# Expert matmuls in plain fp32 on column tiles in place of a three-product split

## What is computed

```
hidden = silu(rows @ w_e_gate[l, e]) * (rows @ w_e_up[l, e])      # 1024 -> 1024
x[picked] += affinity * gate2 * (hidden @ w_e_down[l, e])          # 1024 -> 1024, scatter-add
```

## Time and profile before

| | us |
|---|---|
| median of 3 runs | 2853.08 (2852.55 to 2854.35) |
| profiled execution, its own time | 2853.54 |
| its span in the trace | 2851.5 |
| TensorE busy | 2629.6, 92% of the span |
| mean granted TensorE clock | 0.972 of 2.4 GHz |

### The profile page before, as it was taken

One profiled execution on the slowest core, in us unless ns is written; L12 is line 12 of the kernel. 1 busy time (PEld: TensorE's weight loads), 2 busy tenths in 40 slices (PEclk: granted clock), 3 DMA queues, 4 the chain that ended last, 5 costly groups with the idle time before them and its releaser, 6 DMA issues.

```text
span 2851.5 us, 40451 instructions
## 1 busy us (share of the span) xinstructions
PE 2629.6 (92%) x13576; PEld 1829.0 (64%) x13576; DVE 1933.7 (68%) x2986; ACT 1628.2 (57%) x2399; POOL 477.1 (17%) x359
## 2 busy tenths in 40 slices
PE   7899999999997999999979989999999599999995
PEld 1487676766773666666648767776677366666663
DVE  7743566444357999999955356644535799999995
ACT  6635544454324777777743554544422477777774
POOL 1030002112301211212013000211231112122121
PEclk9899999999998999999989999999999899999997
DMA  9630112121447999999972111211134599999995
GB/s 362 250 93 31 34 44 72 41 67 45 168 162 281 383 379 380 381 376 377 385 243 80 43 34 38 73 47 49 63 130 173 208 375 378 377 384 380 378 383 184
DMA packets 191183, 593.74 MB, mean 208 GB/s; under 512 B 23628, under 2 KB 33674, under 8 KB 191054
## 3 DMA queue, kind: packets, MB, share of 16 engines
q1 hardware_dynamic: 171646, 527.68, 49.9%
q0 software_dynamic: 19408, 64.37, 7.6%
HBM read 566.73 MB, written 25.23 MB: 208 GB/s over the span
## 4 chain that ended last, share of the span: by engine, by line
PE 76%; DVE 9%; ACT 6%; issue 6%; DMA 3%; POOL 0%; ACTq 0%; SPq 0%; DVEq 0%; POOLq 0%
PE bank L530 22%; PE bank L532 20%; PE bank L531 20%; PE bank L941 4%; PE bank L969 3%; DVE low L1554 2%; ACT high L1179 2%; PE bank L956 2%; DMA ring<-in_w_mod 1%; DVE st L1858 1%; PE bank L725 1%; DMA U<-x_normed,idx_g 1%; DVE sigr L1781 1%; PE bank L1090 1%; PE bank L1128 1%
## 5 line engine op out<-in xcount | busy, mean ns | idle before, releaser
L1179 ACT ACTIVATE high<-ring 128x1024 fp32r<-128x1024 f32 (+1 forms) x976 | 1023.8, 1052 | 393.4 <-PE bank L532 359.9
L1994 DVE TENSOR_TENSOR low<-ring,high 128x1024 fp32r<-128x1024 f32 x736 | 880.6, 1220 | 72.6 <-ACT high L1179 69.8
L530 PE MATMUL bank<-high,hT_high 128*128 128x512 f32 (+2 forms) x1280 | 516.5, 404 | 25.4 <-DVE low L1554 9.7
L531 PE MATMUL bank<-low,hT_high 128*128 128x512 f32 (+2 forms) x1280 | 484.3, 378 | 0.0
L532 PE MATMUL bank<-high,hT_low 128*128 128x512 f32 (+2 forms) x1280 | 483.4, 378 | 0.0
L530 PE MATMUL bank<-high,xeT_high 128*80 128x512 f32 x1056 | 419.0, 397 | 5.6 <-issue 3.5
L531 PE MATMUL bank<-low,xeT_high 128*80 128x512 f32 x1056 | 416.6, 394 | 0.0
L532 PE MATMUL bank<-high,xeT_low 128*80 128x512 f32 x1056 | 416.5, 394 | 0.0
L1554 DVE TENSOR_TENSOR low<-ring,high 128x1024 fp32r<-128x1024 f32 (+2 forms) x240 | 285.9, 1212 | 114.0 <-ACT high L1179 112.7
L530 PEld LDWEIGHTS bank<-high,hT_high 128*128 128x128 f32 x1280 | 242.3, 189 | 92.2 <-issue 17.2
L1400 ACT ACTIVATE att<-bank,st 128x640 f32<-128x640 f32 (+3 forms) x200 | 136.4, 682 | 278.9 <-DVE st L1863 220.9
(11 more groups left out here) (261 smaller groups left out, 3164.4 us busy)
## 6 DMA issues: line engine op xcount, KB each, us to landing
ring<-in_w_e_gate SPq DMA_DIRECT2D x256, 512.0 KB, 6.3
ring<-in_w_e_up SPq DMA_DIRECT2D x256, 512.0 KB, 7.0
ring<-in_w_e_down SPq DMA_DIRECT2D x256, 512.0 KB, 6.3
ring<-in_w_mod SPq DMA_DIRECT2D x64, 512.0 KB, 6.5
ring<-in_w_gate SPq DMA_DIRECT2D x64, 512.0 KB, 4.1
ring<-in_w_in SPq DMA_DIRECT2D x24, 512.0 KB, 4.6
U<-in_w_mod SPq DMA_DIRECT2D x20, 512.0 KB, 5.4
ring<-in_w_branch SPq DMA_DIRECT2D x16, 512.0 KB, 4.4
```

What stands on the lines that cost most here:

```text
L530: nc.tensor.matmul(out, lhs[0], rhs_high, start=start, stop=False)
L531: nc.tensor.matmul(out, lhs[0], rhs_low, start=False, stop=False)
L1179: A(high[:, HSLOT[g], :, 0:w], ring[:, SLOT[g], :, 0:w], ACT.Copy).then_inc(high_done, 1)
L1994: V.tensor_tensor(low[:, SLOT[ahead], :, :], ring[:, SLOT[ahead], :, :], high[:, HSLOT[ahead], :, :].bitcast(F32), ALU.subtract).then_inc( ...
```

## The change

Experts no longer split their weights. TensorE multiplies the raw fp32 chunk in plain fp32, and the picked tokens are laid out in two ways over the array's columns: the 64 sample tokens stand in two halves of 64 columns, which take the two halves of a chunk, and the 16 prompt tokens, padded to 32, stand in four strips of 32 columns, which take the four quarters of 256 columns. A chunk is 2 + 4 matmuls in place of 6. Sample results lie in one PSUM bank (partitions 0 to 63 hold the first 512 output columns, 64 to 127 the rest), prompt results in 256 columns of another.

What follows from it: silu, the product and the hidden rows are on 128 partitions with 512 + 256 columns instead of 80 with 2 x 512; the hidden turn is six full transposes instead of eight; the turned rows are copied once by ScalarE, with no low part; the gate values are spread over 128 partitions by small VectorE operations and two more transposes before the stage; GpSimd zeroes the pad; the gate2 row is loaded in six pieces instead of two; the result of an expert is evacuated in two operations on 64 partitions by 512 and four on 16 by 256. The dense part keeps its splits, with four high slots.

```diff
@@ matrix (TensorE)
-                        split_done(g + k, i)
+                        pe.wait_ge(ring_full[SLOT[g + k]], i * (16 * LOOP_FILLS) + 16 * FILLS[g + k])
+                        w = ring[:, SLOT[g + k], :, :]
                         for half in range(2):
-                            ins = three(bank(first + half)[0:CAP, :], stat(k), high[:, HSLOT[g + k], half, :],
-                                        low[:, SLOT[g + k], half, :], k == 0, k == KD - 1)
+                            mm(bank(first)[CAP_S * half:CAP_S * (half + 1), :], stat(k)[0], w[:, half, :], start=(k == 0), stop=(k == KD - 1))
+                        for q in range(4):
+                            ins = mm(bank(first + 1, 0, QW)[STRIP * q:STRIP * (q + 1), :], stat(k)[1],
+                                     w[:, q // 2, QW * (q % 2):QW * (q % 2 + 1)], start=(k == 0), stop=(k == KD - 1))
                         ins.then_inc(ring_used, 1)
@@ hid_turn (TensorE)
-                            for k in range(4):
-                                kk = 4 * half + k
-                                ins = tr(bank(6 + half, k * CAP, (k + 1) * CAP), hid[0:CAP, kk * P:(kk + 1) * P], ident[0:CAP, 0:CAP])
+                            for k in range(4 if half == 0 else 2):
+                                ins = tr(bank(6 + half, k * P, (k + 1) * P), hid[:, half * NW + k * P:half * NW + (k + 1) * P], ident[:, :])
@@ before the first gather (TensorE)
                 pe.wait_ge(topT_ready, l + 1)
+                pe.wait_ge(spread_set, l + 1)
+                for a in range(2):
+                    ins = tr(bank(1, (2 + a) * NE, (3 + a) * NE), spread[:, a, :], ident[0:NE, 0:NE])
+                ins.then_inc(spread_tr, 1)
                 rows_turn(0, 16 * (NE // 2 * l + 1))
@@ experts (ScalarE)
-                    for j in range(6 * NQ):
...
-                        split_high(g + HIGH_E, i)
+                    g = g0 + CH_GATE0 + e * CH_EXP
+                    rows_copy(1 - e, n_exp * 2 + 2)
+                    hid_copy(0, n_exp)
+                    for half in range(2):
+                        silu(half, n_exp + 1, i * (2 * CH_EXP) + (g + 4 * NQ))
@@ before the stage (VectorE)
+                then(V.memset(spread[:, 1, :], 0.0))
+                for half in range(2):
+                    at = slice(CAP_S * half, CAP_S * (half + 1))
+                    V.tensor_copy(spread[:, 0, at], top_v[:, 0:CAP_S])
+                for q in range(4):
+                    at = slice(STRIP * q, STRIP * q + CAP_P)
+                    ins = V.tensor_copy(spread[:, 1, at], top_v[:, CAP_S:CAP])
+                ins.then_inc(spread_set, 1)
+                dve.wait_ge(spread_tr, l + 1)
+                V.tensor_copy(gate_T[:, :, :], bank(1, 2 * NE, 4 * NE).rearrange("p (a n) -> p a n", a=2)).then_inc(spread_done, 1)
@@ experts (VectorE)
-                        chunk_low(g + HIGH_E, i)
...
-                    y_half(0, e, i * (2 * CH_EXP) + (g + 1))
-                    y_half(1, e, i * (2 * CH_EXP) + (g + 1)).then_inc(y_ready, 1)
+                    for half in range(2):
+                        at = slice(CAP_S * half, CAP_S * (half + 1))
+                        V.scalar_tensor_tensor(out=ybuf[0:CAP_S, e, half * NW:(half + 1) * NW], in0=bank(first)[at, :],
+                                               scalar=gate_c[at, e, 0:1], in1=gate2_b[at, 0:NW], op0=ALU.mult, op1=ALU.mult)
+                    for q in range(4):
+                        at = slice(STRIP * q, STRIP * q + CAP_P)
+                        ins = V.scalar_tensor_tensor(out=ybuf[CAP_S:CAP, e, QW * q:QW * (q + 1)], in0=bank(first + 1, 0, QW)[at, :],
+                                                     scalar=gate_c[at, e, 1:2], in1=gate2_b[at, NW:NW + QW], op0=ALU.mult, op1=ALU.mult)
+                    ins.then_inc(y_ready, 1)
@@ before the first gather, and behind both gathers (GpSimd's queue)
+                G.memset(xeT[:, :, :, CAP:WIDE], 0.0).then_inc(pad_zero, 1)
...
-                pool.dma_start(gate2_b[0:CAP_S, :], mod_dram[l, 1:2, 5 * D:6 * D].broadcast_to([CAP_S, D])).then_inc(gate2_in, 16)
-                pool.dma_start(gate2_b[CAP_S:CAP, :], mod_dram[l, 0:1, 5 * D:6 * D].broadcast_to([CAP_P, D])).then_inc(gate2_in, 16)
+                for half in range(2):
+                    pool.dma_start(gate2_b[CAP_S * half:CAP_S * (half + 1), 0:NW],
+                                   mod_dram[l, 1:2, 5 * D + NW * half:5 * D + NW * (half + 1)].broadcast_to([CAP_S, NW])).then_inc(gate2_in, 16)
+                for q in range(4):
+                    pool.dma_start(gate2_b[STRIP * q:STRIP * (q + 1), NW:NW + QW],
+                                   mod_dram[l, 0:1, 5 * D + QW * q:5 * D + QW * (q + 1)].broadcast_to([STRIP, QW])).then_inc(gate2_in, 16)
```

More of the change, by code:

```diff
@@ L26 @@
 CAP = CAP_S + CAP_P
+STRIP = 32
+WIDE = CAP_S + STRIP
+QW = 256
 EPS = 1e-6
@@ L275, in plan_ring @@
         hslot.append(h)
+        last[a] = g
+        if h is None:
+            hfree.append(None)
+            continue
         hfree.append(None if hlast[h] is None else hlast[h] + 1)
-        last[a] = hlast[h] = g
+        hlast[h] = g
     return slot, fills, free, hslot, hfree
@@ L282, with split_no @@
 LOOP_FILLS = 2 * CH_EXP // RING_E
+def split_no(g):
+    if g < CH_MOD:
+        return g
+    l, c = divmod(g - CH_MOD, CH_LAYER)
+    return CH_MOD + l * CH_DENSE + c
 def plan_later():
@@ L1115, in hid_in @@
                 def hid_in(n_exp, half):
-                    return lambda: pe.wait_ge(hidT_low, n_exp * 2 + (half + 1))
+                    return lambda: pe.wait_ge(hidT_ready, n_exp * 2 + (half + 1))
                 def next_turn(e, i):
@@ L1139, in expert @@
                     pe.wait_ge(y_ready, n_exp + 1)
-                    matrix(g + 4 * NQ, i, 4, lambda kk: [t[:, kk, :] for t in hidT], [(0, hid_in(n_exp, 0)), (4, hid_in(n_exp, 1))])
+                    matrix(g + 4 * NQ, i, 4, inner_of(0), [(0, hid_in(n_exp, 1))])
                 def last_two(i):
@@ L1167, in _, with split_high @@
             called = [0]
[L1169 to L1177, removed]
+            def split_high(g):
+                act.wait_ge(ring_full[SLOT[g]], 16 * FILLS[g])
+                if HIGH_FREE[g] is not None:
+                    act.wait_ge(ring_used, HIGH_FREE[g])
                 w = width_of(g)
@@ L1517, in _ @@
+                    rows_copy(1, n_exp * 2 + 2)
+                    hid_copy(0, n_exp)
+                    for half in range(2):
+                        silu(half, n_exp + 1, i * (2 * CH_EXP) + (g + 4 * NQ))
+                    hid_copy(1, n_exp + 1)
+                    if l + 1 < L:
+                        for c in range(HIGH):
+                            split_high(chunk_no(l + 1, c))
                 act.wait_ge(lg_full, l + 1)
-                for j in range(HIGH, HIGH_E):
-                    split_high(g0 + j)
@@ L1520, in _ @@
                 if l == 0:
                     later_out_rows(0)
-                rows_high(0, 2 * NE * l)
+                rows_copy(0, 2 * NE * l)
                 later_out_rows(1 if l == 0 else GAP_FIRST[l])
-                for j in range(CH_GATE0):
-                    split_high(g0 + j + HIGH_E)
                 for half in range(2):
@@ L1923, in _ @@
                         norm_lows(q2, m - 2, 0)
-                for c in range(CH_OUT + NQ, CH_OUT + NQ + T - 3):
-                    split_low(chunk_no(l, c) + HIGH)
                 dve.wait_ge(lg_full, l + 1)
@@ L1955, in _ @@
                     V.tensor_copy(idx_g[:, b, 0:1], idxT[:, b:b + 1]).then_inc(idx_ready, 1)
-                for c in range(CH_OUT + NQ + T - 3, CH_DENSE):
-                    split_low(chunk_no(l, c) + HIGH)
-                def rows_low(b, highs):
-                    for half in range(2):
-                        ks = slice(4 * half, 4 * half + 4)
-                        dve.wait_ge(xe_high, highs + (half + 1))
-                        low_part(xeT[1][:, b, ks, :], bank(6 + half, 0, 4 * CAP), xeT[0][:, b, ks, :], xe_ready)
@@ L1982, in gate_in @@
                     dve.wait_ge(added, n_exp + (BUF - 1))
[L1983 removed]
+                    for a in range(2):
+                        V.tensor_copy(gate_c[:, e, a:a + 1], gate_T[:, a, bass.ds(i * 2 + e, 1)])
                     V.tensor_copy(idx_s[:, e, 0:1], idxT[:, bass.ds(i * 2 + e, 1)]).then_inc(gate_set, 1)
[L1986 to L1990 removed]
@@ new lines, in last_two @@
+                    hid_product(n_exp, i * (2 * CH_EXP) + (g + 2 * NQ))
+                    gate_in(n_exp, 0, i)
+                    hid_product(n_exp + 1, i * (2 * CH_EXP) + (g + 6 * NQ))
+                    gate_in(n_exp + 1, 1, i)
+                    dve.wait_ge(gate_set, n_exp + 1)
+                    y_out_of(0, i * (2 * CH_EXP) + (g + 8 * NQ))
+                    if l + 1 < L:
+                        for c in range(HIGH):
+                            split_low(chunk_no(l + 1, c))
+                    dve.wait_ge(gate_set, n_exp + 2)
```

162 lines of the change are left out of this document (49 added, 113 removed).

## The result

The changed kernel takes 2987.6 us (four runs, 2983.2 to 2988.2) against 2853.7 in the same rounds: 1.0458 times, 95% interval 1.0445 to 1.0471. 2998 was forecast.

A forecast was written before the change was run, and what follows sets the result against it. Matmul issue on TensorE was taken as the bound; 143.0 us for both stages, -1.4 ahead and +3.2 at the ends gave +144.8, so 2998 us, 5.1% slower. Its own range was 2925 to 3100, with rivals 2790 to 3170.

The forecast's parts named there:

- What bounds before: Experts' stage before the change: matmul issue sets the pace, 1.385 us a chunk, not splits or stream.
- The chunk: TensorE's time for one expert chunk after the change: 1.319 us of matmuls plus 0.265 for layout changes, taken as 1.58.
- offsets of 7 and 21 ns: Within a chunk: delays between records that start together, 7 ns in the halves and 21 in the strips.
- The changes of layout: Each chunk goes halves, strips, halves: two drains of 0.095 us and longer first passes of 0.051 and 0.024, 0.265 together.
- The 2.38 times: Prompt strips: the skill's 3/2.38 would lengthen the chunk by 0.11 us, total about 3080; left out of the sum.
- The stage: From first to last expert matmul of a layer: 632.1 us against 560.6, 71.5 more a layer, 143.0 for both.
- the low clock at the start: First matmuls of a layer's experts' stage: the lower clock costs 1.7 us, as before the change.
- The edges: Around the experts' stages: -0.7 us a layer ahead of them, +3.2 in all after the last experts.
- under the gather: Before each stage: eight splits stood within TensorE's 5.02 us idle wait for the gather; removing them wins 0.7 a layer.
- The faster rival: Halves to strips within each chunk costs no drain: chunk 1.30 us, expert about 33.5, total about 2808; chance 0.13.
- The sum of 144.8 us: Whole kernel: 143.0 for the stages, -1.4 ahead of them and +3.2 at the ends, giving +144.8 us.
- The range's lower bound: Forecast's own range starts at 2925 us, from a chunk of 1.48: two drains without load losses and less 0.1.

The follow-up runs named there:

- two strips: Changed kernel with strips 2 and 3 (half of the prompt tokens' columns) left out in seven chunks of eight: 2971.5 us.
- the groups: Changed kernel with the halves of two or four chunks issued first, then their strips, same matmuls: 2878.3 us with two, 2821.4 with four.
- one layout: Changed kernel with the 64 sample tokens also in strips of 32 columns: 2789.3 us, 0.9776 times the kernel before.

## Why the prediction was right, by its own steps

- **What bounds before.** Matmul issue, with splits and stream a little behind: two products instead of three gained 55 us, and then VectorE and the stream were both full. Right.
- **The chunk.** 1.58 forecast, 1.58 measured. Its terms: two passes at once for the halves (0.43 each), four strips at once (two strips gave 14 ns), offsets of 7 and 21 ns, first passes longer by 51 and 24 ns (643 less 592, 403 less 379), and the changes. The weight load of 32 columns, interpolated at 104 ns, is 106 at the least and 109 in the median.
- **The changes of layout.** This was the term without a row: that going from 64-column halves to 32-column strips costs what the other changes cost. Forecast 0.265 a chunk and 0.028 of staggering, 0.293 together; measured 0.285 and 0.296 a round by the groups, and all of it gone with one layout. The Trainium skill's rule (TensorEngine Tiling, Key Properties), that changing the tiling mode drains the engine, agrees with the traces for the kind that the trace of before did not have: from the start of the sample matmuls to that of the strips it is 0.86 us in one layout and 1.01 in two.
- **The 2.38 times** for three column tiles that the Trainium skill measured (TensorE: Matmul & The Clock Gate, Part 3) would, by the prediction's estimate, have put 0.11 on the chunk. The strips' passes show none of it: in a stream of them four tiles give four times, less 21 ns.
- **The stage.** +71.5 a layer forecast, +68.9 and +70.5 measured. An expert takes 39.4 us, as forecast. In the first layer the low clock at the start did not come (-1.7): TensorE was busy in 6.0 of the 7.6 us before the stage, where it had been in 1.3 of 7.0 in the kernel before, and the granted clock is 1.00 from its first chunk.
- **The edges** were the step that was off. Forecast: -1.4 ahead of the stages, as the gather's wait was put down to the gather itself. Measured: -11.1. The row that showed it was on the page already: a gather's issue at a mean of 4.5 us on GpSimd, with one of 0.92 in the timeline right behind it. The prediction called the splits "under the gather" and free; they lengthened it. At the end, +3.2 was forecast for both layers; the narrow evacuations take 0.48 us each, not 0.40, and the last scatter starts 2.1 to 2.2 us later behind each stage. Yet at the first boundary nothing was lost (27.5 us before and after), since that scatter, with the same issue of 1.39 us, landed 1.1 us sooner and the reload behind it was 1.3 us quicker; the end of the kernel grew by 3.3.
- **The faster rival** (no drain) was priced at 2808 for a kernel that then existed only as a thought. The one-layout version has that kernel's chunk (1.29 us), at 2789: the stream could do 394 GB/s, between the bounds of 378 and 410, and an expert took about 32.7 us while the stream was ahead and 33.6 behind it, where 33.5 had been priced.

The sum of 144.8 us stands against 134 in the medians and 129.9 in the traces. Of the 14.9 between sum and traces, the stages are 3.6 and what lies around them 11.3: no large error was balanced by another. The medians came 4 us nearer because the profiled execution was the quickest. The range's lower bound was looser than its words: a chunk of 1.48 is 1.584 less one change of 0.1, while two drains without load losses and less 0.1 would be 1.41.

## What to carry to other kernels

Column tiles in plain fp32 run at full rate beside each other, two or four at a time, so a thin product can be paid for by its columns. But choose one tile width for all products that alternate: here each round of 64-column and 32-column tiles cost 0.29 us, over a fifth of the 1.29 us of work in a chunk, and two 32-column tiles did the work of one of 64 for nothing. When an engine that is off the path is relieved, look at who shares something with it: the splits made TensorE wait 0.3 us before a down matrix and 1.7 before the last one, and some 5 us a layer more through the gather, whose issue they held up by 5.8.

## What the runs showed that I had not expected

- The issue of an indirect gather took 6.8 us under the splits and 0.97 without, and moving six subtractions alone made the kernel before 12 us faster. Added VectorE work of like size gave only 1.1 to 1.9.
- The number of matmuls cost nothing: with one layout a chunk has eight instead of six, and takes 1.29 us instead of 1.58.
- A faster stage gave 9.5 us back at the layer boundary: the last expert's evacuation stood in VectorE's program behind splits whose chunks came late.
